# The scan's inverse: in each pass both directions' first products, then both transposed sums

## The reference, cut to what matters

```python
def _wkv7_scan(r, w, k, v, kk, a):
    def step(state, inp):
        r_t, w_t, k_t, v_t, kk_t, a_t = inp
        sa = jnp.einsum('bhvk,bhk->bhv', state, kk_t)
        state = (state * w_t[:, :, None, :]
                 - sa[..., None] * (kk_t * a_t)[:, :, None, :]
                 + v_t[..., None] * k_t[:, :, None, :])
        return state, jnp.einsum('bhvk,bhk->bhv', state, r_t)
...
y = _wkv7_scan(rh, w_f, kh, vh, kk, ah)
y = y + flip(_wkv7_scan(flip(rh), flip(w_b), flip(kh), flip(vh), flip(kk), flip(ah)))
```

## Time and profile before

| | |
|---|---|
| time, three runs | 3372.6, 3376.15, 3376.59 us; median 3376.15 |
| span of the profiled execution | 3368.4 us (what lies around the span: 7.75 us to the median of the runs) |
| TensorE busy | 3206.5 us, 95% of the span |
| chain that ended last | TensorE 75%, "issue" 10%, VectorE 7%, GpSimd 4%, ScalarE 3% |
| the scan | from 905 to 1245 us of the span: 8 pairs of heads, 40 passes of the inverse of some 3.4 us |

### The profile page before, as it was taken

How to read it: one execution, slowest core, us unless ns; L and a number is a source line. 1 busy time by engine, 2 the same in 40 slices (tenths; PEclk the granted TensorE clock), 3 DMA queues, 4 the chain that set the end, 5 groups by cost and what they waited for, 6 DMA issues and landing times.

```text
span 3368.4 us, 62850 instructions
## 1 busy us (share of the span) xinstructions
PE 3206.5 (95%) x25640; PEld 2434.2 (72%) x25640; DVE 1575.6 (47%) x2342; ACT 1134.2 (34%) x1623; POOL 1203.6 (36%) x612
## 2 busy tenths in 40 slices
PE   7999999979899999999998998989999999999999
PEld 5757888848688887777766856458886774448887
DVE  6755553194255555677130421444152576636060
ACT  5413433222433333444233313232223334622121
POOL 3333444414144412444433412014443264314443
PEclk9999999979899999999999999999999899999999
DMA  3212333313000002555322222112322120013333
GB/s 129 82 44 82 98 95 100 107 52 99 14 3 3 3 9 72 186 186 183 126 96 79 92 65 69 44 62 94 99 95 88 50 75 32 1 62 94 100 94 100
DMA packets 73073, 266.37 MB, mean 79 GB/s; under 512 B 8207, under 2 KB 8218, under 8 KB 72704
## 3 DMA queue, kind: packets, MB, share of 16 engines
q1 hardware_dynamic: 72000, 260.32, 24.2%
q0 software_dynamic: 896, 3.52, 0.3%
HBM read 261.71 MB, written 2.10 MB: 78 GB/s over the span
## 4 chain that ended last, share of the span: by engine, by line
PE 75%; issue 10%; DVE 7%; POOL 4%; ACT 3%; DMA 0%; POOLq 0%; DVEq 0%; ACTq 0%; SPq 0%
PE gp L388 53%; POOL w_low L357 4%; PE gp L1227 4%; PE gp L2174 2%; PE gp L314 2%; PE gp L2678 2%; PE aux L1353 1%; PE aux L1227 1%; PE gp L1985 1%; PE gp L2637 1%; PE gp L2655 1%; PE aux L1994 1%; DVE arena L1667 1%; DVE aux L2858 1%; PE aux L1222 1%
## 5 line engine op out<-in xcount | busy, mean ns | idle before, releaser
L357 POOL TENSOR_TENSOR w_low<-ring,w_high 128x1024 fp32r<-128x1024 f32 x397 | 956.0, 2409 | 1747.2 <-ACT w_high L326 1747.2
L326 ACT ACTIVATE w_high<-ring 128x1024 fp32r<-128x1024 f32 x397 | 420.1, 1059 | 1346.3 <-PE gp L388 1289.1
L388 PE MATMUL gp<-ffn_h,w_high 128*128 128x512 f32 x2432 | 756.8, 393 | 13.0 <-DVE ffn_h L418 5.1
L388 PEld LDWEIGHTS gp<-ffn_h,w_high 128*128 128x128 f32 x2432 | 454.8, 188 | 123.6 <-POOL w_low L357 12.5
L388 PE MATMUL gp<-ffn_h,w_low 128*128 128x512 f32 x1216 | 474.6, 390 | 0.0
L388 PE MATMUL gp<-ffn_high,w_high 128*128 128x512 f32 x928 | 362.0, 390 | 3.0 <-POOL w_low L357 2.8
L388 PE MATMUL gp<-ffn_low,w_high 128*128 128x512 f32 x864 | 336.6, 390 | 0.0
L388 PE MATMUL gp<-ffn_high,w_low 128*128 128x512 f32 x864 | 336.6, 390 | 0.0
L388 PEld LDWEIGHTS gp<-ffn_h,w_low 128*128 128x128 f32 x1216 | 229.1, 188 | 48.3
L2102 DVE TENSOR_TENSOR arena<-arena 128x512 f32<-128x512 f32 x64 | 152.9, 2389 | 200.3 <-ACTq L163 200.3
L388 PE MATMUL gp<-in_h,w_high 128*128 128x512 f32 x768 | 239.6, 393 | 4.4 <-DVE in_h L416 4.2
(11 more groups left out here) (470 smaller groups left out, 5172.1 us busy)
## 6 DMA issues: line engine op xcount, KB each, us to landing
ring<-in_weights SPq DMA_DIRECT2D x437, 512.0 KB, 3.6
H<-in_ada SPq DMA_DIRECT2D x48, 512.0 KB, 4.3
X<-in_x SPq DMA_DIRECT2D x4, 512.0 KB, 7.3
out_x<-X SPq DMA_DIRECT2D x8, 256.0 KB, 4.5
arena<-in_sm POOLq DMA_DIRECT2D x1, 1024.0 KB, 5.0
cst<-in_cst SPq DMA_DIRECT2D x1, 756.0 KB, 9.7
arena<-in_hy_f_w POOLq DMA_DIRECT2D x1, 512.0 KB, 5.4
arena<-in_hy_delta POOLq DMA_DIRECT2D x1, 512.0 KB, 5.9
```

Of the source, the lines that this page charges most:

```text
L326: nc.scalar.activation(w_high[:, slab % PARTS, :], ring[:, slab % RING, :], ACT.Copy).then_inc(high_ready, 1)
L357: nc.gpsimd.tensor_tensor(w_low[:, slab % PARTS, :], ring[:, slab % RING, :], w_high[:, slab % PARTS, :], ALU.subtract).then_inc(low_ready, 1)
L388: last = nc.tensor.matmul(gp[:, t.bank, :], wt[:, slab % PARTS, w], x(k), start=(k == 0 and q == 0), stop=(k == sum(kt) - 1 and q == 2))
```

## The change

In each pass of the inverse, TensorE's order X0, P0, X1, P1, S0, S1 becomes P0, P1, X0, X1, S0, S1. The waits on `rw_tokst` and `rw_XS` stay at the head of the first loop and stand before P0 and P1 now; X0 and X1 have a loop of their own with no wait. Each group keeps its operands, its destination and its semaphore. No other engine's program changes.

```diff
@@ -1349,13 +1349,14 @@
                         pe.wait_ge(rw_tokst, n_tok(it, d))
                         pe.wait_ge(rw_XS, summed)
                         for j, p, h in TILES:
+                            last = quarter_mm(MIDDLE[d][:, half4(p, j)], MB[d][:, j, h, 0:64], XS[d][:, half4(h, j)], p, h)
+                        last.then_inc(rw_T1, 1)
+                    for d in DIRS:
+                        for j, p, h in TILES:
                             out = aux[HEADS[h], 2 * (1 - d) + p, cs(j)]
                             last = nc.tensor.matmul(out, XS[d][HEADS[p], half4(h, j)], const("eye64")[HEADS[p], :],
                                                     start=True, stop=True, skip_group_check=True)
                         last.then_inc(rw_dXT, 1)
-                        for j, p, h in TILES:
-                            last = quarter_mm(MIDDLE[d][:, half4(p, j)], MB[d][:, j, h, 0:64], XS[d][:, half4(h, j)], p, h)
-                        last.then_inc(rw_T1, 1)
                     for d in DIRS:
                         level = lv * 2 + n_lv(it, 0, d)
                         pe.compute_val(level)
```

## The result

The changed kernel takes 3388.6 us (median of five runs, 3386.09 to 3392.31) against 3376.15 (five runs, 3372.6 to 3378.31): a ratio of 1.0038, 95% interval 1.0026 to 1.005, some 12.5 us slower. The forecast was 3386.5 us, with a range of 3379 to 3397.

The account below looks back on a forecast made before the run. TensorE's own path was taken to bound the kernel. Later passes 5.5, last passes 1.6 and first passes 5.0 us made 12.1; less 1.7 given back, +10.4 us, so 3386.5 us, range 3379 to 3397.

Parts of the forecast that it names:

- Bound, and nothing beside it: In the inverse: TensorE's own path sets the end; nothing beside it would hide a longer or shorter inverse.
- The removed hole: Before S1 in each pass: TensorE no longer waits for mask 1, worth 0.33 us a pass.
- Wait B and C: In each pass: S0 waits for copy 0, until X0 + 1.40 us; S1 waits for copy 1, until X0 + 1.90.
- the lag e: Time from copy 0's end to S0's start on TensorE: taken as 0.07 us, bounds 0.05 to 0.09.
- Wait D: At the next pass's start: P0 waits for subtraction 0, starting 1.26 us after S0, at X0 + 2.66.
- Wait A: Early in the pass: P1 waits for subtraction 1, 1.27 us after S1's start, so 0.51 after P0.
- The sum: Over all inverses: later passes 5.5 us, last passes 1.6, first passes 5.0, together 12.1 us before anything is given back.
- What is given back: In six first passes: late-code stalls on "issue" overlap the new waits, hiding up to 3.5 us; half, 1.7, was taken.
- The span: Whole kernel: profiled span 3368.4 us plus 10.4, plus 7.75 between that span and the runs' median, gives 3386.5.
- Only the removed hole counts: Rival, chance 0.05: copy 0 reaches S0 in time, each pass shrinks by 0.33 us, 13.2 us off, 3363 us.
- The late code pays: Rival, chance 0.16: first-pass stalls totalling 5.5 us vanish whole; +5.8 us, 3382 us, within 0.2%.
- Much slower: Rival, chance 0.11: the sequencer's exposed register work and unoverlapped copies cost +17 to +22 us, best 3395 us.

## Why the prediction was right

**Bound, and nothing beside it:** right. All of the 13.3 us lie in the inverses; behind the scan nothing moved (2128.5 and 2128.6), and GpSimd's wait for ScalarE grew with the inverse, from 139.1 us to 151.0.

**The removed hole:** right. The masks are done before S0, and nobody waits for them.

**Wait B and C:** right in place, undersized. S0 starts 1.48 after X0 instead of 1.40. The term that was off is the lag e from the copy's end to S0: I took 0.07, from two other releases, and it measured 0.14, above the upper end of 0.09 that I gave it. The second copy starts 0.49 behind the first (0.50 expected). TensorE's weight loads stand idle for 0.44 us before S0 (0.45 expected), though the timeline puts that idle time down to "issue".

**Wait D:** right in place, undersized for the same reason: the next P0 comes 1.32 after S0, not 1.26, as the subtraction's end frees TensorE after 0.14 where I had put the mask's 0.09.

**Wait A:** right in size, not visible as a wait of its own. P1 starts 0.50 after P0 in the mean of all later passes (0.51 expected) and X0 0.98 after P0 (0.98 expected); but 0.49 is also what a group takes that nothing holds.

**The sum**, by pairs without late code: third pair 19.21 before and 21.28 after (1007.09 to 1028.37), the seventh nearly the same: +2.07. Of this 0.77 is the first pass (0.63 expected), 1.03 the three regular passes together (0.69 expected; over all 24 the mean is 0.36 a pass where I had 0.23), and the remaining 0.27 the last (0.20 expected). Eight pairs would make 16.6 us against my 12.1.

**What is given back:** right that it exists; half of 3.5 us was too little. All eight inverses sum to 161.4 before and 174.7 after, +13.3, so 3.3 us of the 16.6 came back. What is left of the six stalls of the earlier trace rows, in the changed kernel's timeline:

```profile
966.45 0.47 PE L1227 MATMUL gp<-arena 64*64 64x64 f32 x17 [0.61 <-issue]
...
1056.08 0.39 PE L1357 MATMUL aux<-cst,arena 64*64 64x64 f32 x10 [0.20 <-issue]
...
1102.48 0.93 PE L1227 MATMUL gp<-arena 64*64 64x64 f32 x40 [0.29 <-issue]
...
1149.29 0.34 PE L1227 MATMUL gp<-arena 64*64 64x64 f32 x7 [0.42 <-issue]
...
1239.37 0.97 PE L1227 MATMUL gp<-arena 64*64 64x64 f32 x48 [0.36 <-issue]
```

The first pair's stall of 0.87 is gone; the others were 0.65, 0.37, 1.09, 1.10 and 1.38. (Besides them, 0.25 us at the first turn of the sixth pair's loop stands in both kernels.) The prediction asked whether code is asked for before the new waits or only behind them. The new waits don't put it off: counted from the first wide copy of the pair, the packet of instructions that ends such a stall starts within 0.2 us of where it started before, in five of the six pairs. In the second pair it starts 0.5 us later and ends 0.6 later, and that is the stall that hardly shrank. In a first pass S0 now starts 2.88 us into it instead of 1.92, and S1 3.37 instead of 2.69, so a stall in S0 can lose up to 0.96 us and one in S1 up to 0.68, if its packet comes no earlier.

By pairs, 0.16 to 0.85 us came back. So my rule, that each stall hides the smaller of itself and 0.63, was not what happened pair by pair, and that its bound of 3.5 us is close to the 3.3 measured is in part luck. It is luck too that the two errors went opposite ways: 16.6 - 3.3 = 13.3 against 12.1 - 1.7 = 10.4.

**The span:** my 7.75 us "around" the span was no such thing. In the changed kernel's profiled execution, time less span is 3387.09 - 3385.3 = 1.8 us, and the other traces of this study have that too. With 1.8 around it, the profiled execution of before would have taken some 3370.2 us, below each of its five runs. Added to the median of the runs, the sum was unharmed.

**The rivals.** "Only the removed hole counts" would have needed S0 at less than 0.93 after X0; it is at 1.48. "The late code pays" named as its sign a stall shortened by over 0.63 us. That sign came, four times (by 0.87, 0.80, 0.68 and 1.02), but the stalls didn't vanish whole, and what the new waits add was larger than thought. "Much slower" named two prices: uncovered register work shows nowhere (P1 follows P0 without a gap in regular passes), and the copies do overlap.

**What stays open:** why a release by this copy or by the subtraction takes 0.14 us, by the mask 0.09 and by the opening's wide copy 0.05. It is 0.14 in the changed kernel unrolled too (first copy from 922.58 to some 923.18, S0 at 923.32), so expected values in registers aren't the reason. Open too is why the second pair's packet starts later than before. A mask in two halves, to close the hole before S1, was not tried. None of the orders tried is measurably faster than the kernel before.

## What to carry to other kernels

When an in-order engine hands results to others and takes them back, write down for each hand-over the time from the start of the producing group to the start of the freed one (here 1.26, 1.32 and 1.48 us), and order the groups so that the longest has most work in front of it. Grouping like with like, as here, lengthened one distance (P1 to S1) by shortening another (X0 to S0). A hole that a profile shows (0.33 us here) is worth its length only if the new order leaves no other result short of cover; count that for every result, and for the first turn of a loop by itself.

## What the runs showed of the hardware that I had not expected

- Instruction code can be the bound of an engine that issues many small operations: a group of 16 products takes 0.46 us, and code arrived at about one 16 KB packet in 3.6 us (kernel before unrolled). Writing out the five passes of eight pairs added 48 packets and some 75 us.
- TensorE's stalls on "issue" can be tied to their cause: the six of the earlier trace rows and all 54 in the inverses of the kernel before unrolled end 1.2 to 1.6 us behind the end of a 16 KB packet on the queue of instructions.
- Of two ScalarE copies in a row, the second starts 0.10 to 0.11 us before the first has ended (0.49 apart for 0.60, 0.92 apart for 1.02), even if the second has a wait of its own that has been met.
- The lag from an instruction's end to the start of what it frees on TensorE isn't one number: 0.05 to 0.14 us in the same stage. For a step that is repeated forty times that difference is 3.6 us.
